# Layer norm of a convolution branch: the eight channel tiles are added on GpSimd, TensorE sums one tile, and a gate projection stands an iteration sooner

## The reference

```python
def _conv_branch(val, gate, og, conv_k, conv_b, ln_g, ln_b, w_o):
    u = val * jax.nn.sigmoid(gate)
    u = _causal_depthwise_conv(u, conv_k, conv_b)      # 31 taps, 1024 channels
    u = _layernorm(u, ln_g, ln_b, LN_EPS)              # over the 1024 channels
    u = jax.nn.silu(u) * jax.nn.silu(og)
    return u @ w_o
...
        m = jax.nn.sigmoid(g_conv) * y_conv + jax.nn.sigmoid(g_rwkv) * y_rwkv
```

## Time and profile before

| | us |
|---|---|
| device time, median of three | 1071.34 |
| the three | 1070.48, 1071.34, 1071.58 |
| span of the profiled execution | 1069.5 |
| TensorE busy | 1059.4 |
| VectorE busy | 740.0 |
| ScalarE busy | 235.8 |
| GpSimd busy | 122.9 |

### The profile page before, as it was taken

How to read it: one execution, slowest core, us unless ns; L and a number is a source line. 1 busy time by engine, 2 the same in 40 slices (tenths; PEclk the granted TensorE clock), 3 DMA queues, 4 the chain that set the end, 5 groups by cost and what they waited for, 6 DMA issues and landing times.

```text
span 1069.5 us, 21375 instructions
## 1 busy us (share of the span) xinstructions
PE 1059.4 (99%) x8774; PEld 914.2 (85%) x8774; DVE 740.0 (69%) x1684; ACT 235.8 (22%) x621; POOL 122.9 (11%) x172
## 2 busy tenths in 40 slices
PE   9999999999999999999999999999999999999997
PEld 8899899998998689999844888898998989887983
DVE  4477674766744277877756688767778778777885
ACT  4131130312220030010100432323232232324101
POOL 1101000000035311100051000000000000000042
PEclk9999999999999999999999999999999999999999
DMA  7776566452448447564457233333233332161261
GB/s 274 250 277 251 187 219 211 155 212 78 159 130 262 139 138 191 199 204 162 172 182 275 64 115 99 100 100 102 98 100 120 103 96 81 31 248 40 79 158 40
DMA packets 62771, 163.19 MB, mean 153 GB/s; under 512 B 8625, under 2 KB 22865, under 8 KB 62674
## 3 DMA queue, kind: packets, MB, share of 16 engines
q1 hardware_dynamic: 61666, 160.19, 44.7%
q10 hardware_dynamic: 1008, 1.63, 0.4%
HBM read 160.69 MB, written 1.11 MB: 151 GB/s over the span
## 4 chain that ended last, share of the span: by engine, by line
PE 97%; DVE 1%; DMA 1%; issue 0%; ACT 0%; POOL 0%; DVEq 0%; ACTq 0%; POOLq 0%
PE bank L828 23%; PE bank L983 18%; PE bank L480 17%; PE bank L894 6%; PE bank L1009 4%; PE bank L640 3%; PE bank L760 2%; PE bank L803 2%; PE bank L1154 2%; PE bank L1166 2%; PE bank L1323 2%; PE bank L956 1%; PE bank L1045 1%; PE bank L556 1%; PE bank L962 1%; PE bank L1023 1%
## 5 line engine op out<-in xcount | busy, mean ns | idle before, releaser
L983 PE MATMUL bank<-hT,slots 128*128 128x256 f32 x896 | 204.5, 382 | 0.0
L983 PEld LDWEIGHTS bank<-hT,slots 128*128 128x128 f32 x896 | 167.8, 190 | 23.2 <-issue 0.3
L480 PE MATMUL bank<-hT,slots 128*128 128x256 f32 x544 | 119.7, 379 | 0.0
L480 PEld LDWEIGHTS bank<-hT,slots 128*128 128x128 f32 x544 | 103.0, 190 | 14.4 <-issue 0.6
L2433 DVE SCALAR_TENSOR_TENSOR arena<-padA,par,arena 128x256 f32<-128x256 f32 x232 | 102.9, 504 | 0.0
L828 PE MATMUL bank<-arena,slots 128*128 128x128 f32 x768 | 95.6, 275 | 0.0
L828 PE MATMUL bank<-hT,slots 128*128 128x128 f32 x736 | 91.8, 276 | 0.1
L828 PEld LDWEIGHTS bank<-arena,slots 128*128 128x128 f32 x768 | 90.9, 192 | 0.5
L828 PEld LDWEIGHTS bank<-hT,slots 128*128 128x128 f32 x736 | 86.7, 192 | 1.0 <-issue 0.9
L480 PE MATMUL bank<-arena,slots 128*128 128x256 f32 x304 | 66.4, 380 | 0.4 <-DMA slots<-in_w_br 0.4
L480 PEld LDWEIGHTS bank<-arena,slots 128*128 128x128 f32 x304 | 57.5, 190 | 8.8 <-DMA slots<-in_w_br 1.1
(11 more groups left out here) (470 smaller groups left out, 1864.2 us busy)
## 6 DMA issues: line engine op xcount, KB each, us to landing
slots<-in_w_rwkv SPq DMA_DIRECT2D x72, 512.0 KB, 3.6
slots<-in_w_heads SPq DMA_DIRECT2D x68, 512.0 KB, 4.5
slots<-in_w_gu SPq DMA_DIRECT2D x44, 512.0 KB, 4.4
arena<-in_ada_w SPq DMA_DIRECT2D x24, 512.0 KB, 5.2
slots<-in_w_down SPq DMA_DIRECT2D x20, 512.0 KB, 4.0
slots<-in_w_br SPq DMA_DIRECT2D x32, 256.0 KB, 3.1
slots<-in_w_out SPq DMA_DIRECT2D x16, 512.0 KB, 5.0
slots<-in_w_y SPq DMA_DIRECT2D x16, 512.0 KB, 5.5
```

Source lines behind the costliest of these rows:

```text
L480: end = e.matmul(psum, w[:, k * P:(k + 1) * P], rhs[:, k, :], start=k == 0, stop=k == kt - 1)
L983: end = e.matmul(proj(w, q), slot[w][:, k * P:(k + 1) * P], hT[:, k, :], start=k == 0, stop=k == KT - 1)
```

## The change

GpSimd keeps a running sum `csum` of the convolution's tiles: in each iteration, behind its three operations, it waits for `taps.j` and adds `CU[:, j, :]` (in iteration 0 it copies). TensorE's LNSUM is then one matmul of `csum`. The last GRP moves from iteration 8 to iteration 7, ahead of LNVAR in `ORDER`, and ScalarE's gr.7 with it. `early_output(3)` moves from `pe_out` into iteration 8. The two lists of gaps are adapted. From `ORDER` and `read_out` it follows that the last GRP waits for `ln.mean`, and LNVAR for `gc.7`.

```diff
-FILL_LAST = (0, 6, 5, 5, 5, 5, 6)
-FILL_END = (0, 3, 3, 2, 3, 3, 3, 3, 3, 3, 3, 3, 2)
+FILL_LAST = (0, 6, 5, 5, 6, 5, 6)
+FILL_END = (0, 3, 3, 2, 3, 3, 3, 3, 2, 2, 3, 3, 2)
...
-        ORDER += [(w, LAST) for w in (OGP, ROG, LNSUM, GCP, LNVAR, GRP)]
+        ORDER += [(w, LAST) for w in (OGP, ROG, LNSUM, GCP, GRP, LNVAR)]
...
+        def layer_sum(e):
+
+            e.wait_ge(*pool.upto(f"csum.{LAST}"))
+            read_out(e, PLACE[LNSUM, LAST] - 2)
+            e.matmul(proj(LNSUM, LAST), ones, csum, start=True, stop=True).then_inc(*pe.step("ln.sum"))
+            yield
+
+        def layer_squares(e):
+
+            e.wait_ge(*act.upto("ln.sq"))
+            read_out(e, PLACE[LNVAR, LAST] - 2)
             for k in range(KT):
-                end = e.matmul(proj(w, LAST), ones, src[:, k, :], start=k == 0, stop=k == KT - 1)
+                end = e.matmul(proj(LNVAR, LAST), ones, lnq[:, k, :], start=k == 0, stop=k == KT - 1)
...
-                yield from layer_sum(e, LNSUM, CU)
+                yield from layer_sum(e)
                 yield from projection(e, GCP, j)
+                yield from projection(e, GRP, j)
             else:
-                yield from layer_sum(e, LNVAR, lnq)
-                yield from projection(e, GRP, LAST)
-                for m in range(3):
+                yield from layer_squares(e)
+                for m in range(4):
                     yield from early_output(e, m)
...
         def pe_out(e):
-            for m in (3, 4):
-                for _ in early_output(e, m):
-                    pass
+            for _ in early_output(e, 4):
+                pass
...
                     half_gate(GCP, GC[:, j, :], "gc", j)
-                if more:
-                    pass
+                    half_gate(GRP, GR[:, j, :], "gr", j)
             else:
-                half_gate(GRP, GR[:, LAST, :], "gr", LAST)
...
+            e.wait_ge(*dve.upto(f"taps.{j}"))
+            if j == 0:
+                e.tensor_copy(csum, CU[:, 0, :]).then_inc(*pool.step("csum.0"))
+            else:
+                e.wait_ge(*pool.upto(f"csum.{j - 1}"))
+                e.tensor_tensor(csum, csum, CU[:, j, :], ALU.add).then_inc(*pool.step(f"csum.{j}"))
```

## The result

| | before | changed |
|---|---|---|
| device time, median (runs) | 1070.94 (4) | 1077.46 (4) |
| lowest and highest | 1070.48, 1071.58 | 1076.31, 1078.56 |
| span of the profiled execution | 1069.5 | 1076.0 |

What follows compares the result with a forecast made beforehand. The prediction took VectorE's layer norm chain, from F3 to ln.y7, and TensorE's work as equally long, meeting at `conv_pair(0)`. Steps -0.4 plus waits 4.05 give +3.65 us: 1071.34 becomes 1075.0 us, range 1072.7 to 1076.7.

Steps and rivals of the forecast that it cites:

- That ln.y7 is what TensorE meets at `conv_pair(0)`, and that F3 sets it: Output projection start: waits for VectorE's last layer norm product, set by copy F3; TensorE would wait 2.6 us.
- 0.4 us are gained ahead of F3 without new waits: Iterations 7 and 8: steps ahead of VectorE's copy F3 change by +0.43 and -0.86 us, so -0.4 us, not -3.0.
- The three waits: TensorE ahead of F3: GCP for rg.7 0.60 us, GRP for ln.mean 1.24, LNVAR for gc.7 2.2; together 4.05.
- rival A: Waits ahead of F3 cost nothing in the end, each eating the next; 1070.9 us, chance 6%.
- rival D: GpSimd's adds slow VectorE where it has no slack, 0.5 to 0.87 us each; 1076 to 1079 us, chance 7%.
- the rule: SBUF: a two-SBUF-input VectorE instruction contends with a GpSimd SBUF read, one blocking; a collision costs up to a whole add.
- rival E: TensorE's clock falls to 1.2 GHz after new waits of 2.2 and 2.6 us; about 1078 us, chance 2%.
- my signs of being wrong: TensorE enters iteration 8 less than 1 us later than in the kernel before, or ln.y7 ends before 999.
- The base: Whole kernel before: median 1071.34 us, to which the forecast adds; the profiled execution of 1069.5 us stands 1.8 us below.
- the upper bound from the waits: Total time with the waits ahead of F3 at most 4.6 us: 1075.6 us.
- the parts of "slower": Chance of over 1073.5 us, from forecast band, D, E, F and a third of C: 0.82 with rounding.

Runs made afterwards that it cites:

- the balanced one: Changed kernel with steps laid out anew: three last-GRP steps in iteration 7, five in iteration 8, LNVAR behind them, ScalarE's and VectorE's old orders; 1069.77 us, ratio 0.9976.
- the run with the sum alone: Kernel before with only GpSimd's running sum and LNSUM over one tile, other orders old, 25 steps in iteration 7; 1070.18 us, ratio 0.9985.
- the filled gap: Changed kernel with five matmuls nobody reads, ahead of `conv_pair(0)` only; 1077.14 us, ratio 1.0049.

## Why the prediction was right or wrong, point by point

- **That ln.y7 is what TensorE meets at `conv_pair(0)`, and that F3 sets it: right.** TensorE waits 2.36 us there (2.6 forecast), and `conv_pair(0)` starts 9.7 to 9.8 us behind the start of F3's copy in the kernel before, the changed one, the balanced one and those with one or both waits taken away. Filling TensorE's gap with 2.2 us of work left D1 as it was (54.20 against 54.21).
- **That 0.4 us are gained ahead of F3 without new waits: near.** With the two large waits gone D1 is 0.18 us over that of before, and 0.69 us of it are lost to the wait for rg.7 that is left: -0.5 against -0.4.
- **The three waits: right in place and order, near in size.** Counted as in the forecast, from the moment at which the next matmul could have started, rg.7 cost 0.69 us (0.60 forecast), the mean 967.65 - (965.01 + 1.29) = 1.35 (1.24), gc.7 2.46 (2.2). The first two were too small because TensorE started 0.15 us behind VectorE's end and not 0.05; the last because ln.c1 gained only 0.12 us, from 1.33 to 1.21, and not 0.26, when GpSimd was out of its way. Sum 4.5 against 4.05, less 0.4: D1 should be +4.1 and is +3.91, where +3.65 was forecast. An execution without anything else would take 1071.3 + 3.9 = 1075.2 us, and the one of 1075.29 us is that.
- **That the waits add up (rival A): right.** Taking both away brought 3.7 us, one of them 2.2.
- **The adds on GpSimd (rival D): right at nothing,** by a run that has them alone. VectorE is busy 1.8 us longer in iterations 0 to 6 with them (249.85 against 248.07 us), all of it in time that was idle. In each of the iterations 1 to 6 the add falls on one tap of the next tile, which takes 0.70 us instead of 0.41: 0.29 us an add, where I had 0.5. GpSimd's add loses too: it takes 0.84 us there and 0.73 in iteration 7, where VectorE reads PSUM. Without the adds, with them, and two rows of the run with the sum alone:

```profile
676.54 0.41 DVE L2428 TENSOR_SCALAR arena<-padA,par 128x256 f32<-128x256 f32 x1
...
675.64 0.84 POOL L2990 TENSOR_TENSOR arena<-arena 128x256 f32<-128x256 f32 x1 [9.20 <-DVE arena L2438]
675.93 0.70 DVE L2429 TENSOR_SCALAR arena<-padA,par 128x256 f32<-128x256 f32 x1
...
963.79 2.35 POOL L2995 TENSOR_TENSOR arena<-arena 128x1024 f32<-128x1024 f32 x1 [7.04 <-DVE arena L2677]
965.15 2.07 DVE L2692 TENSOR_TENSOR arena<-arena 128x1024 f32<-128x1024 f32 x1
```

  The last row is ln.c1, which began 0.99 us ahead of the end of GpSimd's subtraction and took 2.07 us instead of the 1.21 that it takes when GpSimd is idle. The Trainium skill, SBUF — State Buffer, "Who interferes with whom", has a VectorE instruction with two SBUF inputs contend with a GpSimd one that reads SBUF, and calls the contention an exclusive lock. This row comes near to that, 0.86 of the 0.99 us; ln.c1 in the kernel before (0.12 of 0.25 us) and the tap beside the add lost about half of the overlap. That tap is the first of its tile and has one tensor for input, so it is not of the kind for which the prediction quotes the rule. In the sum-alone run it cost nothing, because ScalarE was squaring the other half of the tiles until 967.23.
- **The clock (rival E): this is the step that failed.** I gave it 2% and left it out of the range, on the ground that the trace has no wait over 1.2 us: but that is just why the trace could say nothing for it, and the change made two waits of twice that length. In four of six profiles with a wait of 2.4 us the clock fell once, behind one such wait, and cost 1.5 to 1.7 us each time, half of the 3 us that I had put down. The forecast needed a term of 0 to 1.7 us, above nothing and never below; with it the range would have gone up to 1078.4. The first profile of the changed kernel is the sum of it: 1071.3 before, 3.9 for the waits, 1.7 for the clock and 0.9 from block 1 make 1077.8 us, and its execution took 1077.75. None of my signs of being wrong came up (ln.y7 ends at 1002.42, far behind 999): they were all about the waits.
- **The base.** Block 1 differs from run to run by up to 3.4 us (the loop starts between 624.92 and 628.28). Neither the median of three before (1071.34) nor that of four after (1077.46) is free of it; measured again, the difference was 4.9 instead of 6.5 us.
- **Two sums of the prediction are slightly off:** the upper bound from the waits is 1075.5 and not 1075.6, and the parts of "slower" add up to 0.84 and not 0.82. Nothing hangs on either.
- **How the 6 us divide in the median.** 3.9 us are the waits, by the trace, by the experiments that take them away and by the second profile of the changed kernel. The clock's part can be read from the mean granted clock of each execution. In the twelve profiles it is 0.996 or 0.997 where the clock fell behind a wait, and 0.998 or 0.999 where it did not (it is under 1 even there, because the clock also falls behind TensorE's last matmul: in the kernel before that one ends at 1062.2, and the granted clock is 0.50 from 1067 to the end). All four executions of the first measurement are at 0.996 or less, so their median has the clock's 1.6 us or so in full. Of the five measured again only the two slowest, 1078.53 and 1080.79, are at 0.996; the other three took 1075.3 to 1076.6 us, and the four with both gaps filled, all at 0.998 or more, 1074.6 to 1077.6. Over all kernels with a wait of 2.4 us, 20 of 38 executions are at 0.997 or less; of the 43 of the other five changed forms none is, and of the 59 of the kernel before that were run beside them one. What is left, some 1 us in either median, is within the spread of block 1 and stays open, and so does what decides in which execution the clock falls.

## What to carry to other kernels

Taking work off the busiest engine pays only where that engine has no appointment further on: look for the engine with which it meets, and count the work removed ahead of the event that sets that engine's chain, not the work removed in all. Where a long operation disappears from a hand-written order, read off what it had been covering, bank by bank, and refill: the same seven steps less cost 6 us in one order and gave 2.6 us (in the trace; 1.7 us by the medians) in another. And a wait of TensorE of 2.4 us had a second price, at the clock, in about half of the executions; the trace of a kernel without such waits can't show it, and that is no reason to put it at nothing.

## What the runs showed of the hardware

- Waits of TensorE of 2.4 us, behind which the granted clock fell to 0.50 (1.2 GHz) in four of six profiles and stayed in two. Each time the fall began only after the wait, once 1.4 us after TensorE had started again at full rate (the filled gap, at 979.4), and the clock was back at 1.00 less than 4 us later. Shorter waits, of 0.7 to 1.2 us in all profiles and one of 1.4 us for a DMA in one, were never followed by it.
- A gap filled with five matmuls of 256 columns that nobody reads is not followed by it either (three of three gaps in front of `conv_pair(0)`, one of one in front of LNVAR), and D1 and D2 show no cost of them.
- VectorE's subtraction of 128x1024 with both inputs in SBUF took 1.21 us when GpSimd was idle, 1.33 us beside the last 0.25 us of GpSimd's and 2.07 us beside the last 0.99 us of it.
